# Moving VectorE's fourth sum and the condition rows, and two opening reorders, in the seven-product tiles of a diffusion trunk

## The chip, the cores and the metric

The kernel runs on one core of one Trainium2 chip. The metric is the device time of one execution in microseconds (us), lower is better; the figure of the kernel before is the median of three runs. In the profile, PE is TensorE (PEld its weight loads), DVE is VectorE, ACT is ScalarE, POOL is GpSimd and SP is SyncE.

## What is computed

One inference step of a two-layer trunk on 128 context and 512 latent tokens (T = 640 columns, model width 1024). Each layer is a half-step FFN, a mixer (attention in layer 0, retention in layer 1) and a second half-step FFN, all modulated by vectors that come from the condition:

```python
def _adaln(cvec, w, b):
    m = jax.nn.silu(cvec) @ w + b
    return m.reshape(cvec.shape[0], 1, N_MOD, D_MODEL)

def _swiglu(h, w13, w2):
    a, b = jnp.split(h @ w13, 2, axis=-1)
    return (jax.nn.silu(a) * b) @ w2

def _ffn_sublayer(x, mod, s, g, w13, w2):
    return x + 0.5 * mod[:, :, 3 * s + 2] * _swiglu(_modulate(x, mod, s, g), w13, w2)
```

The change touches the four FFNs only (D_MODEL 1024, FFN_DIM 2816). All data are float32; every matrix product is made of three products of a high and a low part of each operand (`w2` and `h2` hold both parts, in slots 0 and 1).

## The kernel before

**Tiles.** The kernel is written by hand for each engine: five instruction streams that meet at semaphores, and no scheduler moves anything. FFN q (0 to 3) makes its 22 tiles f of 128 hidden columns in rounds of 6, 6, 6 and 4 tiles (`ROUNDS`), and after each round multiplies the round's tiles with the second weight matrix (the down products, L2509, with the additions into x, L1655 and L1631). The first tiles of an FFN (`CLASSIC`: 4 in FFN 0, 2 in the others) are plain: two weight blocks against h, 96 matmuls of 320 columns on PE (L2379, in `ch_tiles`). All later tiles replace eight half-size block products by seven on sums of the operands.

**A seven-product tile on PE** (`seven_products`, L2476) is seven products m = 0 to 6 of 12 matmuls each, in this order. Product m waits for its left operand's low part. Product 3 also waits for `p_copied`, which says that ACT has copied the results of products 0 and 1 out of PSUM (`first_result` L1006, `second_result` L1013). Product 6 also waits for `v_done`, which is DVE's fourth sum (`fourth_value`, L1806), and that sum needs product 4. PE waits for nothing else in the tile that the change touches.

**DVE in the same tile** first ends the tile before: `first_half_out` (L1813, then L1817) and, once ACT has made the high part (`first_half_high`, L1070), `first_half_low` (L1823). It makes the second, third and fourth sums of this tile (L1783, L1800, L1806), between them the four sums and seven low parts of the next tile's left operands (L1671, L1678, L1685, L1691; L1705, L1700), and at the end the tile's last sum and its product with silu (L1862, L1868, L1873). In the last tile of a round the left operands' work is replaced by splits of down blocks (L1526). A condition row (`ada_blocks`, L1541) is a block of the matrix that makes the modulation vectors, multiplied and summed on DVE; `ADA_UP` says how many of them each tile carries:

```python
ROUNDS = (6, 6, 6, 4)
CLASSIC = (4, 2, 2, 2)
ADA_UP = [[2, 1, 2, 0, 0, 1, 0, 1, 0, 1, 0, 2, 0, 1, 0, 1, 0, 1, 0, 1, 0, 0],
          [0, 0, 0, 0, 1, 1, 0, 1, 0, 1, 0, 0, 0, 1, 0, 1, 0, 0, 0, 1, 0, 0], [0] * FT, [0] * FT]
```

**ACT in the same tile** makes, in a fixed order: `first_half_high` of the tile before (it waits for L1817 on DVE), `first_result` (L1006), the high part 0 of the next tile (L924), `second_result` (L1013), the high parts 1 to 3 (L919), silu (L1092), high parts 4 and 5, silu (L1099), high part 6 and the high part of the tile's output (L1103). In the second seven-product tile of an FFN (`early`) the two results stand ahead of everything else. After the last tile of a round the order is the same with splits of down blocks (L913) in place of the high parts.

**The queues.** SP loads the weight blocks into a ring of four raw buffers and waits for the low part of the block four places back. POOL loads the condition blocks into two buffers; each load waits for the condition row two places back.

Of the kernel before, what the change touches and what calls it, by code (L numbers as in the profile page):

```python
# [18 lines left out]
P = 128  # L19
KD = D // P  # L20
# [111 lines left out]
def chunk(nn, h, k):  # L132

    return 16 * nn + 8 * h + k + 1
# [116 lines left out]
def build(nc, a):  # L251
# [3 lines left out]
    with ctx:  # L255
# [643 lines left out]
        def _(act):  # L899
# [103 lines left out]
            def first_result(sg, s):  # L1003

                act.wait_ge(left_free, 5 * sg + 1)
                act.activation(swu[:, s, :], ps[:, 4 * s, 0:HT], ACT.Copy).then_inc(p_copied, 1)  # L1006
# [53 lines left out]
            def seven_products(q, r, u):  # L1060

                nf, f, n = ROUNDS[r], F0[r] + u, pair_block(q, r, u)
                sg, s = seventh(q, f), u % 2
                d = down_block(q, r, 0)
                last = u + 1 == nf

                def first_half_high(f, u):

                    act.wait_ge(up_free, FT * q + f + 3)
                    act.activation(g2[:, u, 0, 0:HT], tmp_g[:, u % 2, 0:HT], ACT.Copy).then_inc(g_half, 1)  # L1070

                early = u and f == CLASSIC[q] + 1
                if early:
                    first_result(sg, s)
                    second_result(sg, s)
                if u and f > CLASSIC[q]:
                    first_half_high(f - 1, u - 1)
                if f > CLASSIC[q] and not early:
                    first_result(sg, s)
                if last:  # L1080
                    split_in(q, d)
                else:
                    left_high(q, f + 1, n + 2, 0)
                if f > CLASSIC[q] and not early:
                    second_result(sg, s)
                if last:
                    split_in(q, d + 1)
                else:
                    for m in (1, 2, 3):
                        left_high(q, f + 1, n + 2, m)  # L1090
                act.wait_ge(c12_done, sg + 1)
                act.activation(tmp_s[:, s, HT:T], tmp_s[:, s, HT:T], ACT.Silu).then_inc(silu_half, 1)  # L1092
                if last:
                    split_in(q, d + 2)
                else:
                    left_high(q, f + 1, n + 2, 4)
                    left_high(q, f + 1, n + 2, 5)
                act.wait_ge(wt_free, done(n))
                act.activation(tmp_s[:, s, 0:HT], ps[:, 4 * s, 0:HT], ACT.Silu).then_inc(silu_half, 1)  # L1099
                if not last:  # L1100
                    left_high(q, f + 1, n + 2, 6)
                act.wait_ge(g1_done, sg + 1)
                act.activation(g2[:, u, 0, HT:T], tmp_g[:, s, HT:T], ACT.Copy).then_inc(g_half, 1)  # L1103
                if last:
                    first_half_high(f, u)
                    split_in(q, d + 3)
# [405 lines left out]
        def _(dve):  # L1512
# [272 lines left out]
            def seven_products(q, r, u):  # L1785
# [47 lines left out]
                    left_first_sum(*nxt)  # L1833
                if before:
                    first_half_low(f - 1, u - 1)
                ada_blocks(ADA_UP[q][f])
                if not last:
                    left_low(*nxt, 0)
                if not last:
# [7 lines left out]
                    left_low(*nxt, 1)  # L1847
                if not first:
                    third_value()
                if last:  # L1850
                    split(d + 1)
                else:
                    left_third_sum(*nxt)
                    left_low(*nxt, 2)
                if not first:
                    fourth_value()
                if last:
                    split(d + 2)
                else:
# [14 lines left out]
                if last:  # L1874
                    first_half_out(f, n, s)
                    first_half_low(f, u)
                    split(d + 3)

            def ffn(q, l, s):
                nn, n0, xb = NORM_AFTER[q], down_block(q, LAST, 0), FFN_X[q] + 8 * LAST  # L1880
# [469 lines left out]
        def _(pe):  # L2350
# [21 lines left out]
            def ch_tiles(ns, prs, h_wait):  # L2372

                for k in range(KD):
                    h_wait(k)
                    for n, pr in zip(ns, prs):
# [6 lines left out]
                        if k == KD - 1:  # L2383
                            mm.then_inc(wt_free, 1)

            def of_h(k, ri):
                return h2[:, k, ri, :]

# [133 lines left out]
            def ffn(q, nn):  # L2522
                for r, nf in enumerate(ROUNDS):
                    for u in range(nf):
                        f, n = F0[r] + u, pair_block(q, r, u)
                        pe.wait_ge(up_free, FT * q + f + 1)
                        if r and u < 2:
                            pe.wait_ge(x_upd, FFN_X[q] + 8 * r - 2 + 2 * u)
                        if f >= CLASSIC[q]:
                            seven_products(q, r, u)  # L2530
                            continue
                        pe.wait_ge(wt_lo, n + 2)
                        if f == 0:
                            halves((n, n + 1), (0, 1), nn)
                        else:
                            ch_tiles((n, n + 1), (2 * (u % 2), 2 * (u % 2) + 1), lambda k: None)
                    first_two(q, r)
                    if r == LAST:
                        break
                    for m in range(KD):  # L2540
                        have(down_block(q, r, m))
                        if m >= 4:
                            pe.wait_ge(x_upd, FFN_X[q] + 8 * r + m - 3)
                        down_part(q, r, m, m % 4, nf - 1 if m < 2 else 0, nf).then_inc(wt_free, 1)
                nn, n0, xb, nf = NORM_AFTER[q], down_block(q, LAST, 0), FFN_X[q] + 8 * LAST, ROUNDS[LAST]
                for m in range(MH[nn]):
                    have(n0 + m // 2)
                    if m >= 3:
                        pe.wait_ge(x_upd, xb + m - 2)
                    mm = down_part(q, LAST, m, m % 3, nf - 1 if m < 2 else 0, nf)  # L2550
                    if m:
                        mm.then_inc(wt_free if m % 2 else dn_half, 1)
                for h in range(2):
                    for m in range(MH[nn], KD):
                        if h == 0:
                            have(n0 + m // 2)
                            if m < MH[nn] + 3:
                                pe.wait_ge(x_upd, xb + m - 2)
                            else:
                                pe.wait_ge(x_h0, X_H0[nn] + m - 2 - MH[nn])  # L2560
                        elif m >= MH[nn] + 3:
                            pe.wait_ge(x_upd, xb + m - 2)
                        mm = down_part(q, LAST, m, m % 3, 0, nf, h, h + 1)
                        mm.then_inc(wt_free if h and m % 2 else dn_half, 1)
                        if h and m == 5:
                            half_sum(nn, 0)
                        elif h and m == KD - 2:
                            half_rb(nn, 0)
                if q == 3:
                    half_sum(6, 1)  # L2570
                    half_rb(6, 1)
# [691 lines left out]
```

## Time and profile before

| | |
|---|---|
| median of 3 runs | 2902.4 us (2898.78 to 2903.92) |
| profiled execution | 2901.21 us |
| its span, first to last instruction | 2899.4 us |
| granted TensorE clock, mean | 0.996 |
| PE busy | 2851.9 us (98%) |
| DVE busy | 2112.1 us (73%) |
| ACT busy | 1186.0 us (41%) |
| POOL busy | 337.1 us (12%) |

The shares of busy time are means over the whole program. In the seven-product tiles PE is the engine that is to be kept fed, and the times that matter are those at which ACT and DVE deliver what products 3 and 6 wait for. All times in the rows are counted from the span's start. A matmul's end is modelled in the profile, its start is not, so that lateness on PE is best read from the starts.

### The profile page before, as it was taken

The page shows a single profiled execution, that of the slowest core. Times are in us where ns is not written, and L with a number is a line of the kernel's source. Part 1 is how long each engine was busy: PE and PEld are TensorE (multiplying, and loading weights), DVE is VectorE, ACT ScalarE, POOL GpSimd, SP SyncE. Part 2 cuts the span into 40 slices and gives each one's busy share as a digit, 9 for nine tenths or more (in the row PEclk, how much of TensorE's full clock was granted, in tenths as well). Part 3 has the DMA queues.
Part 4 walks back from the last instruction along what each step waited for, and adds up shares of the span by engine and source line. Part 5 has one row for each costly group of instructions (what it writes and reads, how often), then busy time and mean ns, then how long its engine had stood idle before and what let it go on. Part 6 is the DMA issues. An engine that isn't in the chain of part 4 may idle for free. (4 is left out here: it accounts for less than half of the span.)

```text
span 2899.4 us, 46652 instructions
## 1 busy us (share of the span) xinstructions
PE 2851.9 (98%) x18130; PEld 2656.4 (92%) x18130; DVE 2112.1 (73%) x4045; ACT 1186.0 (41%) x2192; POOL 337.1 (12%) x424
## 2 busy tenths in 40 slices
PE   8999999999999999999999999999999999999998
PEld 5999999978789999999999998798887978999998
DVE  5898987766668989778878775755747467866856
ACT  5433535254666334356334353223222134533433
POOL 1000003120030000021000021202111023000001
PEclk9999999999999999999999999999999999999999
DMA  7544343521014443424433323323223231422221
GB/s 258 150 138 135 110 132 115 177 74 50 19 52 131 144 123 100 135 74 115 131 102 99 93 93 104 107 86 124 73 88 109 81 131 37 103 79 88 72 90 66
DMA packets 94237, 303.52 MB, mean 105 GB/s; under 512 B 10752, under 2 KB 21280, under 8 KB 93120
## 3 DMA queue, kind: packets, MB, share of 16 engines
q1 hardware_dynamic: 67328, 223.03, 24.0%
q0 software_dynamic: 21296, 63.58, 8.0%
q10 hardware_dynamic: 5392, 13.92, 1.3%
q8 instruction: 144, 2.36, 0.3%
q14 instruction: 77, 0.63, 0.1%
HBM read 285.14 MB, written 7.49 MB: 101 GB/s over the span
## 5 line engine op out<-in xcount | busy, mean ns | idle before, releaser
L2509 PE MATMUL ps<-g,w 128*128 128x320 f32 x4224 | 625.1, 309 | 1.3 <-DVE x L1655 1.3
L2509 PEld LDWEIGHTS ps<-g,w 128*128 128x128 f32 x4224 | 620.6, 188 | 2.3 <-issue 1.5
L2476 PE MATMUL ps<-h,w 128*128 128x320 f32 x3744 | 580.8, 310 | 9.0 <-DVE swu L1806 7.3
L2476 PEld LDWEIGHTS ps<-h,w 128*128 128x128 f32 x3744 | 556.0, 188 | 13.4 <-DVE swu L1806 9.7
L2476 PE MATMUL ps<-e,w 128*128 128x320 f32 x2808 | 437.2, 309 | 0.0
L2476 PEld LDWEIGHTS ps<-e,w 128*128 128x128 f32 x2808 | 418.2, 188 | 0.0
L1526 DVE TENSOR_TENSOR w<-raw,w 128x1024 fp32r<-128x1024 f32 (+1 forms) x243 | 280.7, 1158 | 158.2 <-ACT w L906 141.2
L2654 PE MATMUL ps<-w,h 128*128 128x512 f32 x1596 | 367.5, 391 | 0.1
L2654 PEld LDWEIGHTS ps<-w,h 128*128 128x128 f32 x1596 | 298.1, 188 | 62.7 <-ACT rg L1470 1.0
L919 ACT ACTIVATE w<-w2s 128x512 fp32r<-128x512 f32 x312 | 193.5, 630 | 261.3 <-DVE w2s L1678 82.1
L906 ACT ACTIVATE w<-raw 128x1024 fp32r<-128x1024 f32 x123 | 128.9, 1061 | 258.6 <-PE ps L2364 131.0
L1705 DVE TENSOR_TENSOR w<-w2s,w 128x512 fp32r<-128x512 f32 x312 | 211.5, 684 | 3.5 <-ACT w L919 2.3
L2364 PE MATMUL ps<-h,w 128*128 128x320 f32 (+1 forms) x1344 | 204.2, 312 | 0.0
L1655 DVE SCALAR_TENSOR_TENSOR x<-ps,gate,x 128x128 f32<-128x128 f32 x216 | 108.4, 545 | 127.4 <-PE ps L2509 114.9
L2364 PEld LDWEIGHTS ps<-h,w 128*128 128x128 f32 x1344 | 199.0, 188 | 1.7 <-issue 1.4
L913 ACT ACTIVATE w<-raw 128x768 fp32r<-128x768 f32 (+1 forms) x120 | 106.0, 886 | 222.8 <-PE ps L2509 191.4
L924 ACT ACTIVATE w<-raw 128x512 fp32r<-128x512 f32 x234 | 145.4, 625 | 72.6 <-PE ps L2509 72.3
L772 POOL DMA_DIRECT2D cond<-in_ada x80 | 43.0, 538 | 945.8 <-DVE acol L1541 939.9
L724 POOL TENSOR_TENSOR tmp_q<-tmp_q 128x320 f32<-128x320 f32 (+1 forms) x72 | 79.2, 1099 | 596.9 <-ACT tmp_q L953 587.7
L2364 PE MATMUL ps<-g,w 128*128 128x320 f32 x912 | 137.4, 313 | 0.9 <-DVE g L2333 0.9
L2364 PEld LDWEIGHTS ps<-g,w 128*128 128x128 f32 x912 | 136.2, 191 | 1.6 <-issue 1.6
L1541 DVE CUSTOM_DVE_ANT_0 unused<-cond,crow 128x512 f32<-128x512 f32 x160 | 110.1, 688 | 6.6 <-DMA cond<-in_ada 2.3
(293 smaller groups left out, 3633.6 us busy)
## 6 DMA issues: line engine op xcount, KB each, us to landing
raw<-in_ws SPq DMA_DIRECT2D x303, 512.0 KB, 3.8
cond<-in_ada POOLq DMA_DIRECT2D x80, 512.0 KB, 3.9
raw<-in_ws SPq DMA_DIRECT2D x96, 384.0 KB, 3.2
raw<-in_ada SPq DMA_DIRECT2D x32, 512.0 KB, 3.6
cond_em<-in_ada POOLq DMA_DIRECT2D x16, 512.0 KB, 3.9
e<-tsum POOLq DMA_DIRECT2D x12, 640.0 KB, 6.3
ada<-in_ada SPq DMA_DIRECT2D x5, 1024.0 KB, 17.9
rst<-in_state ACTq DMA_DIRECT2D x4, 1024.0 KB, 4.9
```

The costliest lines, as they stand in the source:

```text
L906: act.activation(w2[:, slot_of(n), 0, :], raw_of("w", n), ACT.Copy).then_inc(wt_hi, 1)
L913: act.activation(w2[:, slot_of(n), 0, 0:cols], raw_of("w", n)[:, 0:cols], ACT.Copy).then_inc(wt_hi, 1)
L919: act.activation(left(q, f, m, 0), left_value(q, f, m), ACT.Copy).then_inc(left_hi, 1)
L924: act.activation(left(q, f, m, 0), quarter(b, half), ACT.Copy).then_inc(left_hi if m == 0 else wt_hi, 1)
L1526: dve.tensor_tensor(w2[:, slot, 1, 0:cols], raw_of("w", n)[:, 0:cols], w2[:, slot, 0, 0:cols].bitcast(fp32), ALU.subtract).then_inc(wt_lo, 1)
L1541: dve.tensor_tensor_reduce(at if row else spare, at, rows[:, row, c0:c1], 1.0, 0.0, ALU.mult, ALU.add, acol[:, k, to:to + 1]).then_inc(ada ...
L1655: ins = dve.scalar_tensor_tensor(part(xn[:, m, :]), part(pair(pr)), g[:, m, st:st + 1], part(xn[:, m, :]), ALU.mult, ALU.add)
L1705: dve.tensor_tensor(lo, left_value(q, f, m) if m else quarter(n, 0), hi, ALU.subtract).then_inc(left_lo, 1)
L2364: mm = pe.matmul(pair_half(pr, half, width), w2[:, slot, wi, at:at + cols], rhs(k, ri)[:, half * width:(half + 1) * width], start=(k == 0 ...
L2476: mm = pe.matmul(ps[:, 4 * s + bank, 0:HT], w2[:, at // 2, wi, c:c + P], rhs(k, ri), start=start and k + wi + ri == 0, stop=(k == 3 and wi ...
L2509: mm = pe.matmul(pair_half(pr, half), w2[:, slot_of(n), wi, c:c + P], half_of(g2[:, k, ri, :], half), start=k + wi + ri == 0, stop=(k == n ...
L2654: mm = pe.matmul(ps[:, bank_of(t), :], ones_tile(src(k, ri), t), w2[:, slot_of(n), wi, kk * 512:(kk + 1) * 512], start=(k == 0 and ri == 0 ...
```

## The change

Four edits, all in the FFNs.

1. DVE, `seven_products`: `fourth_value` (L1806) stands directly behind `third_value` (L1800); before, the next tile's third left sum (L1691) and one low part (L1705) stood between them.
2. DVE, `seven_products`: the condition rows stand at the end of the tile, behind its last instruction; before, they stood near its start, behind `first_half_low` of the tile before.
3. ACT, `seven_products`: `first_result` and `second_result` of an FFN's second seven-product tile are issued at the end of its first one, ahead of L1103, and no longer at the start of their own.
4. PE, `late_second`: in tile 1 of each FFN the two blocks run three chunks of 6 matmuls apart. PE waits for the first block alone to start, and for the second when those three chunks are issued; before, it waited for both.

```diff
@@ -1070,9 +1070,6 @@
                     act.activation(g2[:, u, 0, 0:HT], tmp_g[:, u % 2, 0:HT], ACT.Copy).then_inc(g_half, 1)
 
                 early = u and f == CLASSIC[q] + 1
-                if early:
-                    first_result(sg, s)
-                    second_result(sg, s)
                 if u and f > CLASSIC[q]:
                     first_half_high(f - 1, u - 1)
                 if f > CLASSIC[q] and not early:
@@ -1099,6 +1096,9 @@
                 act.activation(tmp_s[:, s, 0:HT], ps[:, 4 * s, 0:HT], ACT.Silu).then_inc(silu_half, 1)
                 if not last:
                     left_high(q, f + 1, n + 2, 6)
+                if f == CLASSIC[q] and not last:
+                    first_result(sg + 1, 1 - s)
+                    second_result(sg + 1, 1 - s)
                 act.wait_ge(g1_done, sg + 1)
                 act.activation(g2[:, u, 0, HT:T], tmp_g[:, s, HT:T], ACT.Copy).then_inc(g_half, 1)
                 if last:
@@ -1833,7 +1833,6 @@
                     left_first_sum(*nxt)
                 if before:
                     first_half_low(f - 1, u - 1)
-                ada_blocks(ADA_UP[q][f])
                 if not last:
                     left_low(*nxt, 0)
                 if not last:
@@ -1847,13 +1846,12 @@
                     left_low(*nxt, 1)
                 if not first:
                     third_value()
+                    fourth_value()
                 if last:
                     split(d + 1)
                 else:
                     left_third_sum(*nxt)
                     left_low(*nxt, 2)
-                if not first:
-                    fourth_value()
                 if last:
                     split(d + 2)
                 else:
@@ -1875,6 +1873,7 @@
                     first_half_out(f, n, s)
                     first_half_low(f, u)
                     split(d + 3)
+                ada_blocks(ADA_UP[q][f])
 
             def ffn(q, l, s):
                 nn, n0, xb = NORM_AFTER[q], down_block(q, LAST, 0), FFN_X[q] + 8 * LAST
@@ -2383,6 +2382,27 @@
                         if k == KD - 1:
                             mm.then_inc(wt_free, 1)
 
+            def late_second(ns, prs):
+
+                def chunk(i, k):
+
+                    for wi, ri in ((0, 0), (0, 1), (1, 0)):
+                        for half in range(2):
+                            mm = pe.matmul(pair_half(prs[i], half), w2[:, slot_of(ns[i]), wi, k * P:(k + 1) * P],
+                                           h2[:, k, ri, half * HT:(half + 1) * HT],
+                                           start=(k == 0 and wi == 0 and ri == 0), stop=(k == KD - 1 and wi == 1))
+                    if k == KD - 1:
+                        mm.then_inc(wt_free, 1)
+
+                pe.wait_ge(wt_lo, ns[0] + 1)
+                for k in range(KD + 2):
+                    if k < KD:
+                        chunk(0, k)
+                    if k == 2:
+                        pe.wait_ge(wt_lo, ns[1] + 1)
+                    if k >= 2:
+                        chunk(1, k - 2)
+
             def of_h(k, ri):
                 return h2[:, k, ri, :]
 
@@ -2528,6 +2548,9 @@
                             pe.wait_ge(x_upd, FFN_X[q] + 8 * r - 2 + 2 * u)
                         if f >= CLASSIC[q]:
                             seven_products(q, r, u)
+                            continue
+                        if f == 1:
+                            late_second((n, n + 1), (2 * (u % 2), 2 * (u % 2) + 1))
                             continue
                         pe.wait_ge(wt_lo, n + 2)
                         if f == 0:
```

The first place is DVE's third and fourth sums in tile 7 of FFN 0, the second tile of round 1. Before, on DVE:

```order
L1800 TENSOR_TENSOR tmp_s<-swu,ps 128x320
L1691 TENSOR_TENSOR w2s<-raw 128x512
L1705 TENSOR_TENSOR w_55<-w2s,w_55 128x512
L1806 TENSOR_TENSOR swu<-swu,ps 128x320
L1705 TENSOR_TENSOR w_55<-w2s,w_55 128x512
```

The third sum is L1800, the fourth L1806; a left sum and a low part of 512 columns stand between them. With the change, on DVE, the same place in tile 8 (all tiles inside a round read alike here):

```order
L1800 TENSOR_TENSOR tmp_s<-swu,ps 128x320
L1806 TENSOR_TENSOR swu<-swu,ps 128x320
L1691 TENSOR_TENSOR w2s<-raw 128x512
L1705 TENSOR_TENSOR w_55<-w2s,w_55 128x512 x2
L1860 TENSOR_TENSOR tmp_g<-swu 128x320
```

The fourth sum has passed L1691 and one L1705 (L1860 is the L1862 of before).

The second place is DVE's seam of tiles 7 and 8 of FFN 0, from the last instruction of tile 7, which carries one condition row. Before, on DVE:

```order
L1873 TENSOR_TENSOR g_89<-tmp_g,g_89 128x320
L1813 TENSOR_TENSOR tmp_g<-swu,ps 128x320
L1817 TENSOR_TENSOR tmp_g<-tmp_s,tmp_g 128x320
L1671 TENSOR_TENSOR w2s<-raw 128x512
L1823 TENSOR_TENSOR g_89<-tmp_g,g_89 128x320
L1705 TENSOR_TENSOR w_55<-raw,w_55 128x512
```

Here tile 7's condition row is long done, and `first_half_out` (L1813, L1817) follows the tile's last instruction directly. With the change, on DVE (L1871 is the L1873 of before; the six ISA rows are one condition row):

```order
L1871 TENSOR_TENSOR g_89<-tmp_g,g_89 128x320
L1541 ISA unused_61,acol<-cond_100,crow 128x512
L1541 ISA acol 128x1
L1541 ISA unused_61,acol<-cond_100,crow 128x512
L1541 ISA acol 128x1
L1541 ISA cond_100,acol<-cond_100,crow 128x1024
L1541 ISA acol 128x1
L1813 TENSOR_TENSOR tmp_g<-swu,ps 128x320
L1817 TENSOR_TENSOR tmp_g<-tmp_s,tmp_g 128x320
L1671 TENSOR_TENSOR w2s<-raw 128x512
```

The condition row of tile 7 now stands ahead of L1813 and L1817 of tile 8.

The third place is ACT at the end of FFN 0's first seven-product tile (tile 4) and the start of its second. Before, on ACT:

```order
L1099 ACTIVATE tmp_s<-ps 128x320
L924 ACTIVATE w_55<-raw 128x512
L1103 ACTIVATE g_89<-tmp_g 128x320
L1006 ACTIVATE swu<-ps 128x320
L1013 ACTIVATE swu<-ps 128x320
L1070 ACTIVATE g_89<-tmp_g 128x320
```

The two copies of tile 5's results, L1006 and L1013, come behind the high part of tile 4's output, L1103. With the change, on ACT (L1096 is the L1099 of before):

```order
L1096 ACTIVATE tmp_s<-ps 128x320
L924 ACTIVATE w_55<-raw 128x512
L1006 ACTIVATE swu<-ps 128x320
L1013 ACTIVATE swu<-ps 128x320
L1103 ACTIVATE g_89<-tmp_g 128x320
L1070 ACTIVATE g_89<-tmp_g 128x320
```

The two copies have passed L1103. L1070, `first_half_high`, is where it was; in all later tiles of a round L1006 and L1013 still stand behind it.

## Rows read from the trace of the kernel before

**Rows 1.** The page: PE's granted clock over the span, in 40 slices

```profile
PEclk9999999999999999999999999999999999999999
```

**Rows 2.** Waits of PE: who, for whom, us in total, times, longest

```profile
PE ps L2476 <- DVE swu L1806: 7.3, 9, 1.8
...
PE ps L2379 <- DVE w L1526: 3.1, 4, 0.8
...
PE ps L2476 <- ACT swu L1013: 1.7, 4, 0.4
```

**Rows 3.** Timeline, PE, FFN 1, tiles 2 to 4: start, length, what [idle before]

```profile
896.04 5.44 PE L2476 MATMUL ps<-h,w 128*128 128x320 f32 x36
...
901.32 3.68 PE L2476 MATMUL ps<-e,w 128*128 128x320 f32 x24
...
905.42 2.02 PE L2476 MATMUL ps<-h,w 128*128 128x320 f32 x12 [0.42 <-ACT swu L1013]
...
912.17 3.79 PE L2476 MATMUL ps<-h,w 128*128 128x320 f32 x24 [1.21 <-DVE swu L1806]
...
915.80 3.68 PE L2476 MATMUL ps<-e,w 128*128 128x320 f32 x24
```

**Rows 4.** Timeline, DVE and ACT in the same stretch

```profile
910.04 0.48 DVE L1800 TENSOR_TENSOR tmp_s<-swu,ps 128x320 f32<-128x320 f32 x1
...
911.64 0.48 DVE L1806 TENSOR_TENSOR swu<-swu,ps 128x320 f32<-128x320 f32 x1
...
916.20 0.49 DVE L1817 TENSOR_TENSOR tmp_g<-tmp_s,tmp_g 128x320 f32<-128x320 f32 x1
...
916.72 0.47 ACT L1070 ACTIVATE g<-tmp_g 128x320 fp32r<-128x320 f32 x1 [1.49 <-DVE tmp_g L1817]
...
917.94 0.42 ACT L1013 ACTIVATE swu<-ps 128x320 f32<-128x320 f32 x1
```

**Rows 5.** Timeline, PE and DVE at the start of tile 7, FFN 0; last row tile 9

```profile
187.29 3.68 PE L2476 MATMUL ps<-e,w 128*128 128x320 f32 x24
...
186.33 0.48 DVE L1813 TENSOR_TENSOR tmp_g<-swu,ps 128x320 f32<-128x320 f32 x1
186.84 0.49 DVE L1817 TENSOR_TENSOR tmp_g<-tmp_s,tmp_g 128x320 f32<-128x320 f32 x1
...
188.57 0.69 DVE L1541 CUSTOM_DVE_ANT_0 unused<-cond,crow 128x512 f32<-128x512 f32 x1
...
191.19 0.69 DVE L1705 TENSOR_TENSOR w<-raw,w 128x512 fp32r<-128x512 f32 x1
...
216.08 0.17 DVE L1553 TENSOR_TENSOR mod<-acol,adab 128x16 f32<-128x16 f32 x1
```

**Rows 6.** Timeline, tile 1 of FFN 1 and the start of tile 2

```profile
871.46 0.82 PE L2428 MATMUL ps<-h,w 128*128 128x320 f32 x4
873.07 14.33 PE L2379 MATMUL ps<-h,w 128*128 128x320 f32 x96 [0.79 <-DVE w L1526]
887.24 1.92 PE L2476 MATMUL ps<-h,w 128*128 128x320 f32 x12
...
887.97 1.89 DVE L1705 TENSOR_TENSOR w<-w2s,w 128x512 fp32r<-128x512 f32 x3
```

**Rows 7.** Stages by window: length, busy PE, PEld, DVE, ACT, POOL, clock, DMA

```profile
127.00:131.00 4.00, 2.17 (x15) 1.91 (x15) 3.89 (x7) 1.53 (x3) 0.00 (x0) 1.00 0.83 266
...
2416.00:2418.00 2.00, 1.14 (x4) 1.17 (x5) 1.98 (x4) 2.00 (x4) 0.00 (x0) 0.50 0.00 0
```

**Rows 8.** The chain that ended last, from 2416.86 us: start, length, what

```profile
2416.86 13.14 PE ps L2364 x72
2430.00 10.57 PE ps L2449 x72
```

**Rows 9.** DMA issues on the page: KB each, us to landing

```profile
raw<-in_ws SPq DMA_DIRECT2D x303, 512.0 KB, 3.8
cond<-in_ada POOLq DMA_DIRECT2D x80, 512.0 KB, 3.9
```

## The prediction, on record before the result

> **What bounds the kernel.** The clock row comes first: it is 9 in all 40 slices, so TensorE runs at its upper level practically throughout [rows 1], and what a change can give or cost in the FFNs is idle time of PE. PE's waits come next. Within the edited code there are three kinds: product 6 waits for DVE's fourth sum (9 times, 7.3 us), product 3 for ACT's two copies (4 times, 1.7 us), tile 1 for the low part of its second block (4 times, 3.1 us) [rows 2]. The timeline turns them into lateness. 72 matmuls of 320 columns take 10.57 us back to back [rows 8], so 12 take 1.76, and a tile of seven products 12.32. In FFN 1, product 5 of tile 2 starts at 896.04, so tile 3 starts two products later, at 899.56. Its product 3 is due at 904.84 and starts at 905.42, 0.58 late, where the wait says 0.42. The 24 matmuls from 912.17 to 915.80 take 3.63 us and not 3.52 [rows 3]. So a stall costs its listed idle time plus 0.16 plus 0.10.
>
> By this rule the 13 waits cost 7.3 + 1.7 + 13 x 0.26 = 12.4 us. Seven tiles with a condition row run 0.14 us late below the list's threshold, 1.0 us more. **13.4 us** is all that the seven-product tiles can give: 2.8 in FFN 0's second tile (0.42 and the longest wait, 1.8), 2.2 in each other FFN's second tile, and 4.1 in tiles that carry condition rows. FFNs 2 and 3 lose nothing in any other tile.
>
> **Times that matter in a tile that starts at T.** Product 3 is due at T+5.28, and starts 0.05 after ACT's L1013 ends, so L1013 must end by T+5.23. Product 6 is due at T+10.56 and needs DVE's L1806, which can start when product 4 is done, at T+9.07.
>
> **Edit 1, the fourth sum earlier.** Where DVE is late, L1806 gains two steps of 512 columns, 2 x 0.60. In tile 3 of FFN 1 it ran at 911.64, with L1800 at 910.04; now it starts at 910.44 and ends at 910.92 [rows 4]. Product 6 was due at 899.56 + 10.56 = 910.12, so it is 0.86 + 0.10 = 0.96 late. Where DVE is on time, the edit costs: L1806 waits for product 4 as before, but the two steps now follow it, and the end of the tile comes 1.20 later on DVE. That is what is late next.
>
> **Edit 2, condition rows at the end.** Tile 7 of FFN 0 starts 1.76 before 187.29, at 185.53. DVE starts L1813 at 186.33, T+0.80, and L1817 ends at T+1.80 [rows 5]. With edit 1 all this is 1.20 later: L1817 ends at T+3.00. ACT needs 0.04 and then 1.64 from the start of L1070 to the end of L1013 (916.72 to 918.36 [rows 4]), and in its queue L1006 and L1013 stand behind L1070, which waits for L1817. So without a condition row L1013 ends at T+4.68: 0.55 to spare, hidden by PE's products 0 to 2, and nothing lost. In a round's last tile ACT splits a down block between the copies, 0.2 to 0.4 longer, 0.1 to 0.3 to spare.
>
> Behind a tile with a condition row the row's 2.62 us (188.57 to 191.19 [rows 5]) come ahead of L1813. L1817 ends at T+5.62, L1013 at T+7.30, PE goes on at T+7.35 in place of T+5.28: 2.07 + 0.10 = **2.17 us** late. PE waits, so DVE and ACT catch up within the tile and product 6 costs nothing. The tiles so followed inside a round, from the table of condition rows, are 7, 9, 13, 15 and 19, in FFN 0 and in FFN 1: 10 stalls, 21.7 us. Three of these rows (tile 9 in both, 15 in FFN 1) also close a vector: L1553 at 0.17, its sister L1554 and the gaps, some 0.4 each, an estimate, 1.2 us in all. Rows in a round's last tile (5, 11, 17 in FFN 0, 5 in FFN 1) cost nothing at the end: the first down result is 5.5 products (9.7 us) away; the worst, tile 5 of FFN 0 with 1 + 2 rows and a wait for a condition block, has DVE at its first addition some 14.4 us after the tile, and PE wants it at 21.1. In exchange the stalls of these tiles on product 6, 4.1 us, go.
>
> **Edit 3, the copies of the second tile.** They now run as soon as products 0 and 1 are done, at about T+4.2, so its product 3 is on time. L1103 waits for DVE until later than that anyway and does not move. In FFN 0's second tile the condition row has also gone from before the sums, so its 2.8 us go wholly. In FFNs 1 to 3, 0.96 stays on product 6 (above), and since DVE keeps its times while PE runs 1.20 + 0.32 earlier, tile 4 meets a late L1817: it ends at 916.69 and L1013 at 918.36 [rows 4], against 912.84 + 5.28 = 918.12 for product 3, 0.29 + 0.10 = 0.39 late. 2.2 becomes 1.35 in each. In FFN 1, tile 4 also carries a row, and tile 5 is a round's last: 2.17 + 0.21 = 2.4 us.
>
> **Edit 4, the late second block.** Tile 1 could start at 872.13 and starts at 873.07, when L1526 is done [rows 6]: 0.94 late. The first three chunks of 6 matmuls need 2.64 us of the first block alone, which hides it. In FFNs 0, 2 and 3 I take all of it, 2.8 us. In FFN 1 tile 2 would start at 886.30, its product 1 at 888.06, but DVE's low part for it (first of the three at 887.97) is done at 888.65 [rows 6]: 0.75 is given back, 0.2 stays. Together **3.0 us** (between 0.2 x 4 and 0.94 x 4).
>
> **Queues.** SP reuses a raw block 1.2 to 3.8 us later, and POOL a condition buffer about as much. Both load in under 4 us [rows 9] and the data is wanted a tile or more later; if that cover were gone, a load would cost up to 3.9 us once.
>
> **Sum.** Gone 13.4 and 3.0; new 21.7 + 1.2 + 3 x 1.35 + 2.4 = 29.4. Net 29.4 - 16.4 = **+13.0 us**. On the profiled execution's own 2901.2 that makes 2914.2; it stood 1.2 below the median of 2902.4, and on the median it is 2915.4. I say **2915.0 us**. For the per-stall 0.10 and the slack I allow 11 to 15; the copy chain (1.64) has been seen only behind an early L1070, which is its use here too.
>
> **The rivals.**
>
> *The copies are not held up (faster).* If ACT had L1006 and L1013 out before L1070's wait bites, or DVE reached L1813 behind a row in time, the eleven new stalls would be gone and only 3 x 1.35 stay: 4.05 - 16.4 = -12.3 us, 2890. The point is T+3.51 for the end of L1817; the sum above has it at T+5.62, so 2.1 us of DVE's work ahead of it would have to find idle time. For it: half of the tiles before a row have idle time on DVE. Against: the order rows, which put the row ahead of L1813. Chance 0.07.
>
> *Mixed.* The stalls overlap with waits that DVE has anyway (L1871 for ACT, L1823) and come out at half: 12 less, about 2903, no change. Chance 0.07.
>
> *No slack in the quiet tiles.* Some 60 tiles without a row ahead have L1013 only 0.1 to 0.55 us before its limit. If it came 0.3 later than worked out, the round's last tiles and some of the others would stall by 0.1 to 0.3 each, 4 to 12 us more: 2919 to 2927. Chance 0.09.
>
> *The clock falls.* The stall of 1.8 us in FFN 0 left the granted clock at 1.00, in a stretch with DMA and dense matmuls around it. But at 2416 us, after two stalls with few matmuls between them, it stood at 0.50, the 1.2 GHz level [rows 7], and the 72 matmuls that followed took 13.14 and not 10.57 us, 2.57 more [rows 8]. The new stalls are single ones between dense products, but 2.1 to 2.5 us long, longer than the one that did nothing. If each of 11 cost such a fall, the time would be 2915 + 28 = 2943. The Trainium skill, "TensorE: Matmul & The Clock Gate", section "HAM oscillation — how this bites in real kernels", speaks against this change: idle gaps that recur in a matmul loop can drop the gate to half clock again and again, so that each piece starts slow. By that rule the sum would be near +41, by the row at 127 to 131 us it is +13. Chance 0.05.
>
> **How the numbers follow.** Forecast 0.72; faster rival 0.07, mixed 0.07, quiet tiles 0.09, clock 0.05. A measurement of this kernel tells 0.2%, 5.8 us, from no change. Faster: 0.07. Same: 0.07, and 0.01 from the forecast's lower edge. Slower: 0.85. The range takes in the forecast and most of the quiet tiles' case: 2908 to 2922.
>
> **What would show it.** PE's waits: L2496 (the L2476 of before) waits for ACT's L1013 eleven times for some 2 us, at tiles 8, 10, 14, 16 and 20 of FFNs 0 and 1 and tile 5 of FFN 1, and three times for 0.2; for L1806 only three times, 0.7 each; none in tile 1. In tile 8 L1541 runs before L1813. FFNs 2 and 3 come out about 0.8 + 0.9 us shorter each. Wrong would be a product 3 on time behind a condition row, a clock under 1.00 in an FFN, or stalls in FFNs 2 and 3 beyond tile 4.

## The result, and the profile after

| | before | after |
|---|---|---|
| median | 2902.4 us (6 runs, 2898.78 to 2905.49) | 2923.45 us (6 runs, 2920.82 to 2927.85) |
| ratio, 95% interval | | 1.0075 (1.0065 to 1.0085) |
| profiled execution | 2901.21 us | 2920.9 us |
| its span | 2899.4 us | 2919.1 us |
| mean granted clock | 0.996 | 0.994 |

The change makes the kernel 21 us slower. The prediction said slower by 13, and 2908 to 2922: the sign and the mechanism are as told, and the median lies 1.5 us above the range. One later execution of the kernel before took 7519.05 us; it is left out of every ratio here. Of the page, PE's busy time and the clock:

```profile
PE 2856.3 (98%) x18130; PEld 2662.1 (91%) x18130; DVE 2107.5 (72%) x4045; ACT 1172.9 (40%) x2192; POOL 337.0 (12%) x424
...
PEclk9999999999999999999999999999999999999999
```

The row of the clock reads as in [rows 1], for a slice is 73 us long. PE's busy time rose by 4.4 us (2851.9 before), the span by 19.7: most of the loss is idle time of PE.

PE's waits after (who, for whom, us in total, times, longest). L2496 is the L2476 of [rows 2]:

```profile
PE ps L2496 <- ACT swu L1013: 22.4, 11, 2.4
...
PE ps L2496 <- DVE swu L1806: 2.1, 3, 0.7
...
PE ps L2496 <- DVE w L1705: 0.7, 1, 0.7
```

The wait for ACT's copies went from 4 times and 1.7 us to 11 times and 22.4 us; the wait for the fourth sum from 9 times to 3; and the four waits of tile 1 for L1526 are gone. In their place there is one wait for an L1705, in tile 2 of FFN 1.

One of the eleven in full: the timeline of tile 8 of FFN 0 after the change, which starts at 196.00 minus 12 matmuls, T = 194.24. Columns: start, length, engine, line and operation, and the idle time before it.

```profile
195.83 0.49 DVE L1871 TENSOR_TENSOR g<-tmp_g,g 128x320 fp32r<-128x320 f32 x1
...
196.00 3.68 PE L2496 MATMUL ps<-e,w 128*128 128x320 f32 x24
196.24 0.68 DVE L1541 CUSTOM_DVE_ANT_0 unused<-cond,crow 128x512 f32<-128x512 f32 x1
...
198.85 0.48 DVE L1813 TENSOR_TENSOR tmp_g<-swu,ps 128x320 f32<-128x320 f32 x1
...
199.37 0.49 DVE L1817 TENSOR_TENSOR tmp_g<-tmp_s,tmp_g 128x320 f32<-128x320 f32 x1
...
199.89 0.47 ACT L1070 ACTIVATE g<-tmp_g 128x320 fp32r<-128x320 f32 x1 [4.09 <-DVE tmp_g L1817]
200.27 0.42 ACT L1006 ACTIVATE swu<-ps 128x320 f32<-128x320 f32 x1
...
200.59 0.62 ACT L924 ACTIVATE w<-raw 128x512 fp32r<-128x512 f32 x1
201.10 0.43 ACT L1013 ACTIVATE swu<-ps 128x320 f32<-128x320 f32 x1
...
201.58 2.02 PE L2496 MATMUL ps<-h,w 128*128 128x320 f32 x12 [1.90 <-ACT swu L1013]
```

The condition row holds DVE from 196.24 to 198.85, so L1817 ends at 199.86, which is T+5.62. ACT has been idle for 4.09 us in front of L1070, with two copies queued behind it that it could have made. L1013 ends at 201.53, T+7.29, and PE goes on at 201.58, where 199.52 was due: 2.06 late. The prediction had T+5.62, T+7.30 and 2.07 late.

The same stall in tile 14 of FFN 0 costs more. The timeline of PE there, after the change:

```profile
317.77 2.80 PE L2496 MATMUL ps<-e,w 128*128 128x320 f32 x18
322.48 3.35 PE L2496 MATMUL ps<-h,w 128*128 128x320 f32 x12 [1.90 <-ACT swu L1013]
325.62 2.18 PE L2496 MATMUL ps<-e,w 128*128 128x320 f32 x12
327.64 5.44 PE L2496 MATMUL ps<-h,w 128*128 128x320 f32 x36
```

The idle time is the same 1.90. But product 3 then takes from 322.48 to 325.62, 3.14 us (1.86 in tile 8), and product 4 takes 2.02 us in place of 1.76: **1.54 us** more. The stages of these two tiles by window, after the change (length, busy PE, PEld, DVE, ACT, POOL, granted clock, DMA share, GB/s):

```profile
201.60:205.00 3.40, 3.40 (x23) 3.40 (x24) 2.93 (x6) 2.15 (x4) 0.00 (x0) 1.00 0.24 98
318.60:322.60 4.00, 2.10 (x15) 1.84 (x14) 3.62 (x7) 1.81 (x5) 0.53 (x1) 1.00 0.60 214
322.80:325.80 3.00, 3.00 (x13) 3.00 (x12) 2.23 (x5) 1.40 (x3) 0.00 (x0) 0.50 0.14 56
326.40:330.00 3.60, 3.60 (x27) 3.60 (x26) 2.10 (x5) 1.44 (x3) 0.00 (x0) 1.00 0.02 5
```

Behind the stall of tile 8 the clock stays at 1.00, and 23 matmuls fit into 3.40 us. Behind that of tile 14 it stands at 0.50, the 1.2 GHz level, and only 13 fit into 3.00 us. The stretch at half clock lasts 3.4 us, from 322.8 to 326.2; at 326.4 the clock is back at 2.4 GHz. Five of the eleven stalls have such a fall at their end: tiles 14 and 20 in FFN 0 and tiles 14, 16 and 20 in FFN 1. In the trace before, no FFN tile had one.

So the profiled span divides as follows. The seven-product tiles ran 13.4 us late before. After, they run 38.0 us late, of which 5 x 1.54 = 7.7 is clock and 30.3 is stall. Tile 1 gives 4 x 0.94 = 3.8 back. Outside the FFNs, a half-clock stretch that lay at 2415.2 to 2422.1 before [rows 7] is only 3.4 us long after, from 2439.0, and costs 0.9 less. Another, at 630.1 before, is missing after, but the 0.9 us that it had cost are lost again right behind it, so that it adds nothing. 38.0 - 13.4 - 3.8 - 0.9 = +19.9, against 19.7 measured.

### The profile page after: what moved, and what is told of

It reads as the page before. It is cut to its first block and busy times, and to the rows that moved or that the text cites. A ratio compares the mean times of both kernels' runs of the same rounds, so it can differ in the third digit from the quotient of the medians.

```text
span 2919.1 us, 46652 instructions
## 1 busy us (share of the span) xinstructions
PE 2856.3 (98%) x18130; PEld 2662.1 (91%) x18130; DVE 2107.5 (72%) x4045; ACT 1172.9 (40%) x2192; POOL 337.0 (12%) x424
## 5 line engine op out<-in xcount | busy, mean ns | idle before, releaser
L2496 PE MATMUL ps<-h,w 128*128 128x320 f32 x3744 | 584.7, 312 | 24.9 <-ACT swu L1013 22.4
L2496 PEld LDWEIGHTS ps<-h,w 128*128 128x128 f32 x3744 | 560.0, 189 | 29.5 <-ACT swu L1013 26.6
L2496 PE MATMUL ps<-e,w 128*128 128x320 f32 x2808 | 439.9, 311 | 0.7 <-DVE w L1705 0.7
L2496 PEld LDWEIGHTS ps<-e,w 128*128 128x128 f32 x2808 | 421.3, 189 | 0.9 <-issue 0.9
L1526 DVE TENSOR_TENSOR w<-raw,w 128x1024 fp32r<-128x1024 f32 (+1 forms) x243 | 279.1, 1157 | 151.5 <-ACT w L906 140.5
L1705 DVE TENSOR_TENSOR w<-w2s,w 128x512 fp32r<-128x512 f32 x312 | 206.9, 685 | 2.8 <-ACT w L919 1.7
```

Source lines behind the costliest of these rows:

```text
L1526: dve.tensor_tensor(w2[:, slot, 1, 0:cols], raw_of("w", n)[:, 0:cols], w2[:, slot, 0, 0:cols].bitcast(fp32), ALU.subtract).then_inc(wt_lo, 1)
L1705: dve.tensor_tensor(lo, left_value(q, f, m) if m else quarter(n, 0), hi, ALU.subtract).then_inc(left_lo, 1)
L2496: mm = pe.matmul(ps[:, 4 * s + bank, 0:HT], w2[:, at // 2, wi, c:c + P], rhs(k, ri), start=start and k + wi + ri == 0, stop=(k == 3 and wi ...
```

## The experiments

None of the kernels leaves work out: they differ in order alone. The first four ran with 27 runs of the kernel before beside them (median 2901.74), the other four with 20 (median 2902.75).

### Two copies ahead of the wait

The change, with `first_result` and `second_result` of every tile ahead of `first_half_high`:

```diff
-                if u and f > CLASSIC[q]:
-                    first_half_high(f - 1, u - 1)
                 if f > CLASSIC[q] and not early:
                     first_result(sg, s)
+                    second_result(sg, s)
+                if u and f > CLASSIC[q]:
+                    first_half_high(f - 1, u - 1)
...
-                if f > CLASSIC[q] and not early:
-                    second_result(sg, s)
```

> The changed kernel, but ACT issues first_result and second_result (L1006, L1013) ahead of first_half_high (L1070) in every tile. Theory A (the new loss is the copies queued behind first_half_high, which waits for DVE behind a condition row; the clock falls only because of these stalls): all eleven waits of product 3 for L1013 vanish, L1013 ends at T+4.2 in every tile, product 6 keeps 0.9 us in the second tile of FFNs 1 to 3 and 0.4 us in tiles 10, 10 and 16, no clock fall inside an FFN; 3.8 us of lateness is left in place of 38.1, so about 13.4 - 3.8 + 3.0 = 12.6 us faster than before the change, some 2890 us. Rival B (a condition row at the end of a tile costs its 2.6 us of DVE wherever the copies stand, so DVE is late for product 6 instead): the waits move to L1806, some 10 x 2 us, about 2915 to 2923 us. Rival C (the clock falls for another reason than the stalls): falls at tiles 14, 16 and 20 stay, 8 us, about 2898 us.

Measured: 2890.12 us (5 runs, 2886.29 to 2891.99), ratio 0.9957 (0.9945 to 0.9970). PE's waits of this kernel (L2495 is L2496, L1805 is L1806):

```profile
PE ps L2495 <- DVE swu L1805: 2.3, 4, 0.7
...
PE ps L2495 <- DVE w L1704: 0.7, 1, 0.7
```

No wait for L1013 is left. The timeline of tile 8 of FFN 0 in this kernel shows why:

```profile
196.00 0.44 ACT L1006 ACTIVATE swu<-ps 128x320 f32<-128x320 f32 x1 [0.40 <-PE ps L2495]
196.04 0.68 DVE L1540 CUSTOM_DVE_ANT_0 unused<-cond,crow 128x512 f32<-128x512 f32 x1
...
197.76 0.44 ACT L1013 ACTIVATE swu<-ps 128x320 f32<-128x320 f32 x1 [1.32 <-PE ps L2495]
...
199.32 1.92 PE L2495 MATMUL ps<-h,w 128*128 128x320 f32 x12
...
199.70 0.47 ACT L1070 ACTIVATE g<-tmp_g 128x320 fp32r<-128x320 f32 x1 [1.50 <-DVE tmp_g L1816]
```

The condition row stands where the change put it, and L1070 comes as late as before in the tile. But both copies are out by 198.20, inside ACT's idle time, and product 3 starts at 199.32 with no wait. The seven-product tiles are 5.0 us late in all (3.8 had been expected, without the 0.90 of tile 2 named below). In the profiled execution (2886.43 us, the second fastest of the five) the clock does not fall anywhere in an FFN; its mean is 0.998. So DVE's new order costs the time only through ACT's queue behind it. This version beats both kernels, the one before by 11.6 us. What is left of lateness is 0.96 in each second tile of FFNs 1 to 3, 0.90 in tile 2 of FFN 1, and 1.2 in three tiles behind a closing vector, where product 6 waits. The same order of the copies in the kernel before was not run, so how much of the 11.6 us it would give without the other four edits is open.

### Condition rows back at the start

The change without edit 2:

```diff
                     first_half_low(f - 1, u - 1)
+                ada_blocks(ADA_UP[q][f])
...
                     split(d + 3)
-                ada_blocks(ADA_UP[q][f])
```

> The changed kernel with edit 2 undone: condition rows stand near the tile's start again, edits 1, 3 and 4 stay. Theory A (the rows' place makes the loss): stalls of 2.1 us are gone; behind a tile with a row product 3 is 0.2 to 0.4 us late (ten times), product 6 0.2 late in tiles 9 and 15 with a vector, 1.8 in FFN 0's tile 5, 0.9 in each later FFN's second tile; sum 11.0 us against 13.4 before, with 3.0 us from tile 1: about 5 us faster than before the change, 2897 to 2898 us, no clock fall in an FFN. Rival (edit 1 makes the loss by itself, since everything behind the fourth sum is 1.2 us later): 10 stalls of over 1 us stay and the time is at or over 2905 us.

Measured: 2897.2 us (11 runs), ratio 0.9989 (0.9980 to 0.9998). PE's waits:

```profile
PE ps L2496 <- DVE swu L1806: 4.6, 5, 1.7
```

The long waits for L1013 are gone; the tiles behind a row start product 3 0.15 to 0.3 late, the worst 0.5. The seven-product tiles are 12.8 us late, against 13.4 before. With the other three edits in place, then, edit 2 is what turns the package from slightly faster to clearly slower: 2923.45 - 2897.2 = 26 us. This difference and that of the next experiment overlap, for edit 1 lengthens the stalls that edit 2 makes; they must not be added.

### The fourth sum back

The change without edit 1:

```diff
                     third_value()
-                    fourth_value()
...
                     left_low(*nxt, 2)
+                if not first:
+                    fourth_value()
```

> The changed kernel with edit 1 undone: the fourth sum stands behind the third left sum and low part again, edits 2, 3 and 4 stay. Theory A: each stall behind a row shrinks by the 1.20 us of two steps, from 2.17 to 0.97 (1.38 where the row closes a vector), product 6 of the second tile is 2.1 late again in FFNs 1 to 3; lateness 18.4 us, against 13.4 before, 3.0 us back from tile 1: +2 to +3 us, 2905 us. Theory on the clock (it falls only behind stalls near 2 us or over, by chance of where they meet the chip's watch): no fall in an FFN, so 18 us less than the changed kernel. Rival (it falls at any repeated stall): three or more falls stay, 1.5 us each, 2909 us or more.

Measured: 2907.36 us (11 runs), ratio 1.0022 (1.0013 to 1.0031). PE's waits:

```profile
PE ps L2497 <- ACT swu L1013: 9.3, 11, 1.2
...
PE ps L2497 <- DVE swu L1806: 6.2, 4, 1.9
```

The same eleven stalls cost 0.97 us each (1.37 to 1.44 where a vector closes, 1.20 in tile 5 of FFN 1), 1.2 shorter than with edit 1: the two steps of 512 columns that edit 1 pushes behind the fourth sum. None of these shorter stalls has a fall of the clock behind it. Product 6 is 2.06 late in the second tiles of FFNs 1 to 3, and one of these three has one. So neither expectation on the clock came in full: not the one of no fall in an FFN, with 2905 us, nor the rival's three or more, with 2909. The tiles are 22.3 us late where 18.4 was expected. Of the 3.9 us more, 1.5 is the fall, 0.9 is tile 2 of FFN 1, which the expectation counts with tile 1, and 0.8 is tile 6 of FFN 0, behind two rows. The timeline of PE in tile 3 of FFN 1 and of FFN 2:

```profile
912.31 5.32 PE L2497 MATMUL ps<-h,w 128*128 128x320 f32 x24 [1.90 <-DVE swu L1806]
...
1357.77 3.78 PE L2497 MATMUL ps<-h,w 128*128 128x320 f32 x24 [1.90 <-DVE swu L1806]
```

The wait is the same, 1.90 us; the 24 matmuls behind it take 5.32 us in one tile and 3.78 in the other.

### The late second block alone

Edit 4 in the kernel before.

```diff
+                        if f == 1:
+                            late_second((n, n + 1), (2 * (u % 2), 2 * (u % 2) + 1))
+                            continue
```

> The kernel before with edit 4 alone, the second block of tile 1 three chunks late. Theory A: tile 1 starts 0.94 us earlier in all four FFNs; in FFN 1 tile 2 gives back 0.84 on product 1, where it waits for the low part L1705: 2.9 us faster, 2899.5 us. Rival (ACT or DVE sets the pace of the first tiles, so the gain is eaten in all FFNs): within 1 us of before.

Measured: 2899.42 us (11 runs), ratio 0.9993 (0.9984 to 1.0002). Every tile is as late as in the kernel before but tile 2 of FFN 1, which is 0.91 late. So the edit gives 4 x 0.94 - 0.91 = 2.85 us, where 3.0 was worked out, and the medians differ by 2.3. By its interval alone that is not told from nothing.

### The fourth sum alone, and the copies alone

Edit 1 alone in the kernel before:

```diff
                     third_value()
+                    fourth_value()
...
-                if not first:
-                    fourth_value()
```

> The kernel before with edit 1 alone, the fourth sum directly behind the third. Theory A: 11.0 us of lateness in place of 13.4 (product 6 gains up to 1.2 where DVE is late, product 3 loses 0.2 to 0.4 behind each row tile): 1.7 to 2.4 us faster, 2899.5 to 2900.5 us. Rival (moving the two steps behind the fourth sum costs in every tile): slower than before by 3 us or more.

Edit 3 alone in the kernel before:

```diff
-                if early:
-                    first_result(sg, s)
-                    second_result(sg, s)
...
+                if f == CLASSIC[q] and not last:
+                    first_result(sg + 1, 1 - s)
+                    second_result(sg + 1, 1 - s)
```

> The kernel before with edit 3 alone, the copies of the second tile issued at the end of the first. Theory A: product 3 of the second tile comes on time, 0.58 us and the 0.10 behind it, but DVE's fourth sum keeps its clock time, so product 6 waits that much more: 2.06 in place of 0.58 + 1.38, nothing gained but some 0.1 in each FFN; same as before. Rival (each stall counts by itself): 0.68 x 4 = 2.7 us faster.

Measured: edit 1 alone 2900.57 us (ratio 0.9992, 0.9983 to 1.0001), edit 3 alone 2903.48 us (ratio 1.0002, 0.9992 to 1.0011), 11 runs each. Neither interval excludes no change. With edit 1 alone, the tiles are 12.0 us late in place of 13.4. It shortens the waits on product 6, from 9 and 7.3 us to 2 and 1.9 in the list, and brings small ones on product 3 (PE's waits of that kernel):

```profile
PE ps L2475 <- ACT swu L1013: 2.0, 5, 0.4
PE ps L2475 <- DVE swu L1806: 1.9, 2, 1.0
```

With edit 3 alone product 3 of the second tile is on time and product 6 takes the whole wait. PE's timeline in tile 3 of FFN 1 and the window behind it:

```profile
913.01 5.32 PE L2476 MATMUL ps<-h,w 128*128 128x320 f32 x24 [1.90 <-DVE swu L1806]
```

```profile
914.00:917.00 3.00, 3.00 (x13) 3.00 (x12) 2.99 (x6) 0.47 (x1) 0.00 (x0) 0.50 0.26 33
```

In the kernel before two shorter waits stood here, 0.42 and 1.21 [rows 3], and the clock stayed up. Joined into one of 1.90, the wait has a half-clock stretch behind it in the second tiles of FFNs 1, 2 and 3. A larger stall in FFN 0 (product 6 of tile 5, 2.68 late) has none. The tiles are 17.6 us late in all, of which three falls make 4.6: without the clock, 13.0 against 13.4 before. Edit 3 alone moves the wait from product 3 to product 6 and gains nothing.

### The change once more, and its stalls joined in pairs

The first is the change unaltered: are the falls at fixed tiles? The second moves the condition rows of tiles 9 and 15 onto tiles 7 and 13 in FFNs 0 and 1, so that four pairs of stalls become four long ones:

```diff
-ADA_UP = [[2, 1, 2, 0, 0, 1, 0, 1, 0, 1, 0, 2, 0, 1, 0, 1, 0, 1, 0, 1, 0, 0],
-          [0, 0, 0, 0, 1, 1, 0, 1, 0, 1, 0, 0, 0, 1, 0, 1, 0, 0, 0, 1, 0, 0], [0] * FT, [0] * FT]
+ADA_UP = [[2, 1, 2, 0, 0, 1, 0, 2, 0, 0, 0, 2, 0, 2, 0, 0, 0, 1, 0, 1, 0, 0],
+          [0, 0, 0, 0, 1, 1, 0, 2, 0, 0, 0, 0, 0, 2, 0, 0, 0, 0, 0, 1, 0, 0], [0] * FT, [0] * FT]
```

> The changed kernel once more, for a second profile. Theory on the clock (a stall near 2 us between dense products meets the chip's watch or not, by its phase in that execution): the eleven stalls come out the same to 0.02 us, but the falls to half clock lie behind other stalls and are another number, 2 to 8 in place of 5, 1.5 us each; the time varies run to run by several us more than that of the first experiment does. Rival (the falls belong to the program's places): the same five stalls are followed by a fall. Median 2920 to 2926 us.

> The changed kernel with the rows of tiles 7 and 9, and of 13 and 15, put together on tiles 7 and 13 in FFNs 0 and 1; the same rows in all. Theory A: stalls of 2.17 at tiles 10 and 16 go, those at tiles 8 and 14 grow by a row's 2.62, to 4.8 (5.2 where a vector is closed); lateness without falls some 32 us against 30.3 in the changed kernel, +2 us. Theory on the clock: a stall of about 5 us is followed by a fall each time, four of four, so at least 6 us more; 2921 to 2929 us. Rival (a stall's length doesn't matter): falls behind at most two of the four.

Measured: the change again 2926.17 us (5 runs, 2923.15 to 2930.83), ratio 1.0087 (1.0073 to 1.0101); paired 2927.89 us (4 runs), ratio 1.0089 (1.0075 to 1.0103). The first is at the upper edge of the expected 2920 to 2926, the second within 2921 to 2929.

In the change's second profile the stalls are the same, 22.5 us in 11 waits:

```profile
PE ps L2496 <- ACT swu L1013: 22.5, 11, 2.4
```

Again five have a fall behind them, and four of the five are the same (tiles 14 and 20 in both FFNs); but tile 5 of FFN 1 has one now, and tile 16 of FFN 1 has none. The first two windows of that execution show both, the third another stretch at half clock, 6.8 us long, in the attention between FFNs 0 and 1, where the first profile has none:

```profile
943.80:947.00 3.20, 3.20 (x12) 3.20 (x13) 0.53 (x1) 0.60 (x1) 0.00 (x0) 0.50 0.64 192
1172.60:1176.20 3.60, 1.46 (x10) 1.19 (x9) 3.14 (x9) 1.52 (x4) 0.53 (x1) 1.00 0.47 142
640.00:646.80 6.80, 6.18 (x38) 4.49 (x35) 3.45 (x14) 2.53 (x8) 4.47 (x8) 0.50 0.14 41
```

And PE's timeline in tile 16 of FFN 1 of the same execution:

```profile
1176.37 2.02 PE L2496 MATMUL ps<-h,w 128*128 128x320 f32 x12 [2.32 <-ACT swu L1013]
1178.23 1.92 PE L2496 MATMUL ps<-e,w 128*128 128x320 f32 x12
```

This stall is 2.32 us idle, longer than most; the clock is at 1.00 through it, and the 12 matmuls behind it start 1.86 us before the next product, at full speed. So a stall of this length makes a fall possible, and the execution decides whether it comes. The second profile's span is 2.2 us longer than the first's with as many falls in the FFNs (38.2 us late there against 38.0); PE loses 1.9 us against the first where that third window lies. The 11 executions of the change in the two sets line up by their mean granted clock, which counts falls wherever they are:

| mean clock | spans, us |
|---|---|
| 0.994 | 2919.0, 2919.1, 2919.7 |
| 0.993 | 2921.3 |
| 0.992 | 2923.4, 2923.6, 2924.1, 2924.3, 2925.3, 2926.1 |
| 0.990 | 2929.0 |

With pairs, PE waits 26.2 us in 7 waits:

```profile
PE ps L2496 <- ACT swu L1013: 26.2, 7, 5.2
```

PE's timeline in tile 8 of FFN 0, and two windows behind the long stall in tile 8 of FFN 1:

```profile
205.42 3.30 PE L2496 MATMUL ps<-h,w 128*128 128x320 f32 x12 [5.16 <-ACT swu L1013]
```

```profile
1031.00:1034.00 3.00, 2.36 (x9) 2.36 (x10) 2.70 (x5) 2.11 (x5) 0.00 (x0) 0.50 0.32 128
1034.00:1037.00 3.00, 3.00 (x13) 3.00 (x13) 0.68 (x2) 0.73 (x2) 0.00 (x0) 0.50 0.00 0
```

The four long stalls are 4.75 us idle (tile 14 of FFN 0) and 5.16 (the three others). All four come with a fall, where the rival allowed two; two of them with one of 6.8 us in place of 3.4, and two of the three that stayed at 2.1 to 2.3 have one too. Fewer stalls, each more surely with a fall and sometimes with a longer one: the time comes out as before the pairing.

## Why the prediction was right, and where it was not

**Bound and due times: right.** PE is the engine to be fed, and "L1013 must end by T+5.23" decided each of these tiles. L1817 ends at T+5.62 behind a row, as worked out from [rows 4, 5].

**Edits 1 and 2: right, to the term.** Ten stalls were to cost 21.7 + 1.2 = 22.9 us. Without the clock they cost 11.2 in FFN 0 (2.16 four times, 2.57 in tile 10) and 11.7 in FFN 1 (2.16 three times, 2.65 and 2.58 behind a closing vector), 22.9 in all. For tile 16 of FFN 1 the second profile is taken, where no fall covers it. The runs without edit 2 and without edit 1 confirm the two parts: without the row no long stall, without the two steps each stall 1.20 shorter. The round's last tiles with rows cost nothing, as said; tile 6 of FFN 0, behind two rows, is 0.11 late, which was not foreseen.

**Edit 3: right.** 3 x 1.35 = 4.05 was worked out; 0.95 and 0.40 in each of three FFNs were measured. (In the working of tile 4, "1.20 + 0.32 earlier" doesn't fit its own start of 912.84, which is 1.20 before the 914.04 of the kernel before (915.80 - 1.76 [rows 3]); the sum goes by 912.84.) Tile 5 of FFN 1 costs 2.38, where 2.4 was said.

**Edit 4: right but for a size.** 0.75 was to be given back in FFN 1, and 0.91 was: product 1 is 0.84 late and the product behind it another 0.07, the restart's extra that had been left out. Net 2.85 and not 3.0.

**The sum without the clock:** 22.9 + 4.05 + 2.38 + 0.11 - 13.4 - 2.85 = +13.2, against +13.0 predicted.

**The step that failed: the clock's term, left at zero in the sum.** The prediction took the fall of the clock as a rival that comes behind all eleven stalls or behind none, gave it 0.05, and so left it out of the range. What the runs show is a mixture: 5 of 11 in either profile. Its price was mis-sized too: 2.6 us a fall, from the 72 matmuls of [rows 8], in a half-clock stretch of 6.8 us; here a stretch is 3.4 us long and costs 1.54. The trace before had short ones too, outside the FFNs. Its windows, which the prediction doesn't use:

```profile
43.00:46.30 3.30, 3.07 (x12) 3.07 (x12) 2.46 (x9) 3.20 (x10) 1.63 (x2) 0.50 0.92 333
630.10:633.40 3.30, 3.30 (x21) 2.41 (x22) 3.18 (x10) 1.57 (x5) 1.37 (x4) 0.50 0.17 40
```

The second of them cost 0.9 us. 5 x 1.54 less the 0.9 at 2439 is +6.8 on the profiled execution, and 13.2 + 6.8 = 20.0 against 19.7. The median lies 2.5 us above the profiled execution, where 1.2 had been allowed for. The table of clocks and spans says that the longer executions had more half clock; where, no profile of them shows, and the second profile had its extra outside the FFNs. The prediction did name "a clock under 1.00 in an FFN" as a sign of being wrong, and that sign came five times. The argument against the rival was one stall, that of 1.8 us idle in tile 5 of FFN 0 with the clock at 1.00 [rows 7]. It was short evidence twice over: the new stalls are longer, as the prediction itself wrote, and one case without a fall says little of something that comes in half of the cases. The Trainium skill, "TensorE: Matmul & The Clock Gate", section "HAM oscillation — how this bites in real kernels", which the prediction held against the change, names the mechanism; its own example has waits of about 3 to 5 us ahead of every piece, longer than these stalls. The trace agrees that recurring gaps bring the half clock back again and again, but behind 5 of 11, and for 7.7 us and not the 28 that the prediction worked out by it.

**The rivals.** "The copies are not held up" asked for an L1817 by T+3.51, and it came at T+5.62. Its time, 2890, is what the kernel with both copies ahead of L1070 then took, by another way to the same end. "Mixed" is excluded by the eleven full stalls. "No slack in the quiet tiles" is excluded too: of some 60 tiles without a row ahead, one (0.11) was late. "The clock falls" is the one that came, in part.

**Which stalls have a fall.** Length plays a part: in the seven-product tiles of the ten profiled executions no stall of under 1.89 us idle has a fall at its end; of the 32 stalls of 1.89 to 2.52 us that wait for L1013 or L1806, 16 have one (5 of 11, 5 of 11, 3 of 4, 1 of 3, 2 of 3); and the four of 4.75 and 5.16 us all have. What parts the 32 can be read from the same traces. Within each execution the starts of all falls lie on one even beat, to 0.03 us. Laid on the beat of its own execution, each of the 16 stalls with a fall has its idle time between two beats (at most 0.13 us of it lies outside), and each of the 16 without is cut by a beat (0.17 to 1.07 us lie on the shorter side). That fits the theory put on record for the second profile, that the stall's place in time decides and not its place in the program: tile 16 of FFN 1 had 2.32 us idle in both profiles, all but 0.13 between two beats in the first, and cut in the second. It is a reading of 32 stalls; no run moved a stall against the beat to test it, and what sets the beat is open.

## What to carry to other kernels

When work is moved to the end of a stage on one engine, look for an instruction in a second engine's queue that waits for the result behind it, and for what stands behind *that* instruction: here the idle time of the third engine came from two copies that needed nothing of DVE. Moving them ahead of the wait turned a loss of 21 us into a gain of 12, with the same order on DVE. And price a stall of TensorE not by its idle time alone: give the fall of the clock its own term, with a share of cases between none and all, as soon as the new stalls are longer than any that the trace shows to be harmless.

## What the runs showed of the hardware

- One stall of 1.90 us idle between dense float32 products can leave TensorE at half clock for 3.4 us (0.50 from 322.8 to 326.2 us), which costs 1.54 us on top. It did so behind 5 of 11 stalls of 1.90 to 2.39 us in each of two executions, at four tiles in both and at a fifth that differed.
- Of 32 stalls of 1.89 to 2.52 us in five executions, the 16 with a fall have their idle time, but for 0.13 us at most, between two beats of the even beat on which the falls of their execution start; the 16 without are cut by a beat, with 0.17 us or more on either side.
- Two waits of 0.42 and 1.21 us in one tile did nothing to the clock; joined into one of 1.90 they brought the half clock in three FFNs of three in one kernel, and in one of three in another.
- Stalls of 4.75 to 5.16 us idle came with half clock for 3.4 us in two cases (4.75 and 5.16) and for 6.8 us in the two others (both 5.16).
- A stall costs 0.26 us more than its listed idle time when the clock stays up: 1.90 idle is 2.06 late at product 3, and 2.16 by the tile's end.
